# Two transformer blocks with a routed mixture of experts: the experts' weights dealt to the partitions in runs of 16 and 8 KB

## The reference, cut to what matters

```python
h2 = _rms(x, norm2_g[l]) * (1.0 + sc2[:, None, :]) + sh2[:, None, :]
x = x + g2[:, None, :] * _hier_moe(h2, w_rg[l], b_rg[l], w_re[l], b_re[l], w1[l], w3[l], w2[l])

def _hier_moe(h, w_rg, b_rg, w_re, b_re, w1, w3, w2):
    g_logits = hf @ w_rg + b_rg          # 4 groups
    e_logits = hf @ w_re + b_re          # 16 experts, 4 in a group
    ...                                  # best group, best two of its experts, softmax weights
    for e in range(N_EXPERTS):
        he = jax.nn.silu(hf @ w1[e]) * (hf @ w3[e])
        y = y + combine[:, e:e + 1] * (he @ w2[e])
```

## Time and profile before

| | |
|---|---|
| median of 3 runs | 1717.02 us (1716.3 to 1721.85) |
| the profiled execution, its own time | 1726.32 us |
| its span, first to last instruction | 1724.5 us |
| mean granted TensorE clock | 0.978 |
| PE / DVE / ACT / POOL busy | 94% / 40% / 15% / 6% |
| HBM read / written | 355.02 MB / 15.48 MB |

### The profile page before, as it was taken

How to read it: one execution, slowest core, us unless ns; L and a number is a source line. 1 busy time by engine, 2 the same in 40 slices (tenths; PEclk the granted TensorE clock), 3 DMA queues, 4 the chain that set the end, 5 groups by cost and what they waited for, 6 DMA issues and landing times.

```text
span 1724.5 us, 17356 instructions
## 1 busy us (share of the span) xinstructions
PE 1626.6 (94%) x6960; PEld 878.5 (51%) x6960; DVE 697.5 (40%) x1322; ACT 256.0 (15%) x576; POOL 108.3 (6%) x123
## 2 busy tenths in 40 slices
PE   4999999999999999999989999999989958998997
PEld 2445556474444444446756788448855633333332
DVE  1617853468886000112264765004484342111112
ACT  3121113010000000000154110000222311011110
POOL 1000001100000000001000100001131110110101
PEclk9999999999999999999989999999999978999999
DMA  9452441146665321107610699424623449999996
GB/s 340 169 195 99 146 165 56 49 147 219 214 225 207 135 98 49 49 1 257 225 50 1 229 333 363 175 98 154 197 98 122 147 178 354 390 392 391 391 387 254
DMA packets 160623, 333.94 MB, mean 194 GB/s; under 512 B 15288, under 2 KB 15568, under 8 KB 160544
## 3 DMA queue, kind: packets, MB, share of 16 engines
q1 hardware_dynamic: 141408, 298.90, 47.7%
q0 software_dynamic: 18224, 30.78, 5.5%
q10 hardware_dynamic: 912, 3.17, 0.5%
HBM read 355.02 MB, written 15.48 MB: 215 GB/s over the span
## 4 chain that ended last, share of the span: by engine, by line
PE 88%; DMA 4%; DVE 4%; issue 2%; POOL 1%; ACT 1%; SPq 0%; DVEq 0%; ACTq 0%; POOLq 0%
PE psum L624 85%; PE psum L628 4%; DMA wring<-in_ev_w_in 2%; DMA wring<-in_w_mod 1%; DMA wring<-in_mlp_w 1%; ACT wide L1663 0%; POOL small L1523 0%; DVE wide L2068 0%; DVE big L2401 0%; DMA x_slots<-wide,slot_i 0%; DVE big L2560 0%; DMA big<-x_slots 0%; DVE small L2559 0%; POOL x_slots L1609 0%; DVE small L2183 0%
## 5 line engine op out<-in xcount | busy, mean ns | idle before, releaser
L624 PE MATMUL psum<-wring,big 128*128 128x512 f32 (+2 forms) x1600 | 559.6, 579 | 13.8 <-issue 13.3
L624 PE MATMUL psum<-wide,wring 128*128 128x256 f32 (+3 forms) x1872 | 490.2, 437 | 0.2
L624 PEld LDWEIGHTS psum<-wring,big 128*128 128x128 f32 (+1 forms) x1600 | 242.8, 173 | 310.1 <-issue 306.1
L624 PEld LDWEIGHTS psum<-wide,wring 128*128 128x128 f32 (+1 forms) x1872 | 304.3, 184 | 173.0 <-issue 144.6
L624 PE MATMUL psum<-wring,wide 128*128 128x512 f32 (+3 forms) x576 | 216.1, 576 | 9.0 <-DMA wring<-in_w_mod 5.4
L1663 ACT ACTIVATE big<-psum 128x512 f32<-128x512 f32 (+2 forms) x155 | 83.0, 546 | 665.0 <-PE psum L624 614.3
L2068 DVE SCALAR_TENSOR_TENSOR wide<-wring,csilu,wide 128x512 f32<-128x512 f32 x252 | 175.5, 748 | 3.0
L624 PEld LDWEIGHTS psum<-wring,wide 128*128 128x128 f32 (+1 forms) x576 | 97.7, 188 | 109.2 <-issue 96.0
L2168 DVE TENSOR_TENSOR wide<-psum,gate 128x512 f32<-128x512 f32 x27 | 18.7, 691 | 325.2 <-PE psum L624 325.0
L1523 POOL TENSOR_TENSOR small<-small 128x1 f32<-128x1 f32 (+2 forms) x30 | 41.1, 1372 | 1037.8 <-DVE small L2185 884.7
L1663 ACT ACTIVATE wide<-psum 128x256 f32<-128x256 f32 (+2 forms) x114 | 46.0, 418 | 313.3 <-PE psum L628 158.9
(11 more groups left out here) (266 smaller groups left out, 885.5 us busy)
## 6 DMA issues: line engine op xcount, KB each, us to landing
wring<-in_mlp_w SPq DMA_DIRECT2D x32, 2048.0 KB, 8.7
wring<-in_w SPq DMA_DIRECT2D x32, 2048.0 KB, 21.9
wring<-in_w_mod SPq DMA_DIRECT2D x24, 2048.0 KB, 13.0
big<-in_w SPq DMA_DIRECT2D x23, 2048.0 KB, 20.6
wide<-in_w SPq DMA_DIRECT2D x14, 2048.0 KB
wring<-in_w_ada SPq DMA_DIRECT2D x12, 2048.0 KB, 8.6
wring<-in_w_in SPq DMA_DIRECT2D x8, 2048.0 KB, 8.4
wring<-in_ev_w_in SPq DMA_DIRECT2D x6, 2048.0 KB, 13.0
```

The costliest lines, as they stand in the source:

```text
L624: return nc.tensor.matmul(o, a, b, start=first, stop=last)
```

## The change

The rows of D are dealt to the partitions in another order: partition p gets the rows 8p to 8p + 7 (`(p k) n -> p k n`) of w1 and w3, one run of 16 KB, and of w2, for each half of the 512 inner rows, the two rows 2p and 2p + 1, a run of 8 KB. So that sums run over matching rows, the tokens' columns (`rms_row(t, True)`), the router weights, the modulation (`modp`, a copy of 16 columns of `modc` made through DRAM) and the inner rows `he` take the same order. The core of the diff:

```diff
+        modp = sb("modp", [P, 2, KC])
+        modp_scratch = nc.dram_tensor("modp_scratch", [2, D], F32, kind="Internal").ap()
+            def by_halves(w):
+                return w.rearrange("p (h c) n -> p h c n", h=2)
@@ load_up
-  sp.dma_start(w13_ring[e % 2][:, w], src[0, e].rearrange("(k p) n -> p k n", p=P)).then_inc(...)
+  sp.dma_start(w13_ring[e % 2][:, w], src[0, e].rearrange("(p k) n -> p k n", p=P)).then_inc(...)
@@ load_down
-  sp.dma_start(w2_ring[:, e % 2], I["w2_2"][0, e].rearrange("(f p) n -> p f n", p=P)).then_inc(...)
+  sp.dma_start(by_halves(w2_ring[:, e % 2]), I["w2_2"][0, e].rearrange("(h p c) n -> p h c n", h=2, c=2)).then_inc(...)
@@ load_spill_up, load_spill_down: the same
@@ gpsimd, after pool.wait_ge(x_ready, 12)
+  pool.wait_ge(modc_ready, 4)
+  for j in range(2):
+      pool.dma_start(modp_scratch[j].rearrange("(k p) -> p k", p=P), modc[:, 2, 24 + 8 * j:32 + 8 * j, 0],
+                     allow_slow_non_contiguous=True).then_inc(modp_out, 16)
...
-  (wr[:, :, 0:4], I["w_rg_2"][0].rearrange("(k p) n -> p k n", p=P)),
-  (wr[:, :, 4:20], I["w_re_2"][0].rearrange("(k p) n -> p k n", p=P)),
+  (wr[:, :, 0:4], I["w_rg_2"][0].rearrange("(p k) n -> p k n", p=P)),
+  (wr[:, :, 4:20], I["w_re_2"][0].rearrange("(p k) n -> p k n", p=P)),
...
+  pool.wait_ge(modp_out, 32)
+  pool.dma_start(modp[:, :, :], modp_scratch.rearrange("j (p k) -> p j k", p=P)).then_inc(modp_in, 16)
@@ modulate("moe") and modulate_group on ACT and DVE: modp in place of modc, and once
+  act.wait_ge(modp_in, 16)          # and dve.wait_ge(modp_in, 16)
@@ rms_row
-  signal(v_.tensor_scalar(xn[:, t, :], x, lnr, None, ALU.mult), xn_ready)
+  dst = xn[:, t, :]
+  if dealt:
+      dst, x = dst.rearrange("p (k q) -> p k q", k=KC), x.rearrange("p (q k) -> p k q", k=KC)
+  signal(v_.tensor_scalar(dst, x, lnr, None, ALU.mult), xn_ready)
@@ the unit loop on DVE
-  v_.tensor_tensor(he[:, i % 2, :], sg[:, i % 2, :], psum[:, i % 2, T:2 * T], ALU.mult).then_inc(he_ready, 1)
+  v_.tensor_tensor(he[:, i % 2, :].rearrange("p (c q) -> p c q", c=2),
+                   sg[:, i % 2, :].rearrange("p (q c) -> p c q", c=2),
+                   psum[:, i % 2, T:2 * T].rearrange("p (q c) -> p c q", c=2), ALU.mult).then_inc(he_ready, 1)
```

More of the change, by code:

```diff
@@ L484, in build @@
         modc_ready = sem("modc_ready")
+        modp_out = sem("modp_out")
+        modp_in = sem("modp_in")
         gkw_ready = sem("gkw_ready")
@@ L592, in build, with shift_of, scale_of @@
                  "moe": (2, 1, 0, 0, 2, 4)}
+        def shift_of(part, k):
+            l, half, v = PARTS[part][:3]
+            return modp[:, 0, k:k + 1] if (l, half) == (2, 1) else modc[:, l, 24 * half + k, v:v + 1]
+        def scale_of(part, k):
+            l, half, v = PARTS[part][:3]
+            return modp[:, 1, k:k + 1] if (l, half) == (2, 1) else modc[:, l, 24 * half + 8 + k, v:v + 1]
         def banks_of(part):
@@ L1448, in load_up @@
                 for w, src in enumerate((I["w1_2"], I["w3_2"])):
-                    sp.dma_start(w13_ring[e % 2][:, w], src[0, e].rearrange("(k p) n -> p k n", p=P)).then_inc(w13_in[e % 2], 16)
+                    sp.dma_start(w13_ring[e % 2][:, w], src[0, e].rearrange("(p k) n -> p k n", p=P)).then_inc(w13_in[e % 2], 16)
             def load_down(e):
@@ L1694, in modulate @@
                 act.wait_ge(modc_ready, done)
+                if (l, half) == (2, 1):
+                    act.wait_ge(modp_in, 16)
                 width, per = n * P, 4 // n
@@ L1701, in modulate @@
                         last = f(hT[:, k, at:at + width], bank(name)[:, j * width:(j + 1) * width], ACT.Identity,
-                                 bias=modc[:, l, 24 * half + k, v:v + 1], scale=modc[:, l, 24 * half + 8 + k, v:v + 1])
+                                 bias=shift_of(part, k), scale=scale_of(part, k))
                     free(last, name)
@@ L1986, in modulate_group @@
                     last = f(slots_of(g)[:, k, :], psum[:, 4, k * P:(k + 1) * P], ACT.Identity,
-                             bias=modc[:, 2, 24 + k, 0:1], scale=modc[:, 2, 32 + k, 0:1])
+                             bias=modp[:, 0, k:k + 1], scale=modp[:, 1, k:k + 1])
                 last.then_inc(hs_ready, 1)
@@ L2140, in modulate @@
                 l, half, v, at, n, done = PARTS[part]
+                if (l, half) == (2, 1):
+                    dve.wait_ge(modp_in, 16)
                 width, per = n * P, 4 // n
@@ L2147, in modulate @@
                         last = v_.tensor_scalar(hT[:, k, at:at + width], bank(name)[:, j * width:(j + 1) * width],
-                                                modc[:, l, 24 * half + 8 + k, v:v + 1],
-                                                modc[:, l, 24 * half + k, v:v + 1], ALU.mult, ALU.add)
+                                                scale_of(part, k), shift_of(part, k), ALU.mult, ALU.add)
                     free(last, name)
@@ L2200, in head_rate, with rms_row @@
                 root(v_.tensor_scalar(out_rate, out_rate, 1.0 / width, eps, ALU.mult, ALU.add), out_rate)
-            def rms_row(t):
+            def rms_row(t, dealt=False):
                 x = xres[:, X0 + t, :]
@@ L2725, in _ @@
                     residual(2, "out2", half, (X0 + t,), alpha=1.0)
-                rms_row(t)
+                rms_row(t, True)
             modulate("moe")
@@ L2822, in modulate_group @@
                 for k in range(4, KC):
-                    last = v_.tensor_scalar(slots_of(g)[:, k, :], psum[:, 5, (k - 4) * P:(k - 3) * P], modc[:, 2, 32 + k, 0:1],
-                                            modc[:, 2, 24 + k, 0:1], ALU.mult, ALU.add)
+                    last = v_.tensor_scalar(slots_of(g)[:, k, :], psum[:, 5, (k - 4) * P:(k - 3) * P], modp[:, 1, k:k + 1],
+                                            modp[:, 0, k:k + 1], ALU.mult, ALU.add)
                 last.then_inc(hs_ready, 1)
```

6 lines of the change are left out of this document (3 added, 3 removed).

## The result

| | before | after |
|---|---|---|
| median, same chip | 1718.57 us (1716.3 to 1721.85, 4 runs) | 1749.41 us (1748.72 to 1753.6, 4 runs) |
| ratio | | 1.0173, 95% interval 1.0145 to 1.02 |
| profiled execution / its span | 1726.32 / 1724.5 us | 1748.72 / 1746.9 us |
| mean granted TensorE clock | 0.978 | 0.972 |

Slower by 1.7%, where 0.6% faster was forecast. The page of the profile after: TensorE's line, DMA share and GB/s by slice, the packets, and two of the costliest groups.

What follows compares the result with a forecast made beforehand. TensorE was taken to bound most of the kernel, nearly level with DMA in the experts' stretch. Weight waits -10.7 us and strided pass +0.5 gave -10.2 from 1717.02: 1706.8 us, 0.6% faster, range 1703 to 1721.

Steps and rivals of the forecast that it cites:

- The bound and its relief: Experts' stretch: TensorE needs 247.3 us, DMA takes 259; longer runs remove most of 11.7 us of weight waits, -10.7 us.
- the straight line through 2 and 4 KB: DMA packet cost in the experts' stretch: 11.1 ns fixed plus 73.6 ns for each 2 KB.
- The rival: Experts' stretch: long weight packets hold up the short packets of ysb's store; +14 us, 1731 us, chance 0.14.
- the same 30.0: Experts' stretch: q0's 10.09 MB and what they disturb take 30.0 us of DMA time, before and after alike.
- 21.5 us as the point from which it decides: Experts' stretch: store landing time beyond which VectorE waits; 23 us for two units less 1.5 for work and issue.
- The unit of 13.25 us: Experts' stretch: time of a unit if stores landed in 25 us, against 12.07; 25 us over 21 units.
- the 11 us taken off for a lag: Experts' stretch: VectorE may lag 11 us once before TensorE notices, subtracted from 25 us to give +14.
- The tokens' order: Last pass of `rms_row` reads `x` at a stride of 8 elements: +0.5 us once, bounds 0 and +1.8.
- The inner rows: `he` in the experts' loop reads at a stride of 2 elements; covered even at three times its time: 0.
- GpSimd's stream: Modulation copy ahead of the root for `ikd`: issues 2.5 us later, cover 5.3, so 0; upper end 3.5 us, chance 0.07.
- The tail: After the experts: last pieces of TensorE and VectorE unchanged, the last store only quicker: 0.

Runs made afterwards that it cites:

- e1: Changed kernel with loads of w1, w3 and w2 cut to 4 KB runs, old store of ysb kept; 1719.48 us, ratio 0.9988 to the kernel before.
- e4: Changed kernel with loads of w1 and w3 cut to 8 KB runs, w2 left at 8 KB, old store; 1721.1 us, ratio 1.0005 to the kernel before.
- e3: Changed kernel, long runs kept, with the store of ysb issued as two plain DMAs; 1711.14 us, ratio 0.9951 to the kernel before.
- b1: Kernel before the change with only the store of ysb issued as two plain DMAs; 1716.21 us, ratio 0.9957 to the kernel before.
- e2: Changed kernel with w1 and w3 cut to 2 KB runs and w2 to 4 KB, old store; 1729.68 us, ratio 1.0038 to the kernel before.
- h1: Changed kernel, long runs, two plain stores, modulation copy moved later on GpSimd; 1713.27 us, ratio 0.9944 to the kernel before; repeat 1710.81 us, 0.9929.
- h2: Changed kernel with 4 KB runs, two plain stores and the modulation copy moved later on GpSimd; 1711.16 us, ratio 0.9924 to the kernel before.

## Why the prediction was wrong

**The bound and its relief: right.** TensorE and DMA were nearly level, and with dealt weights the waits for w1 and w3 go from the stretch (11.7 us to none). Its worth of -10.7 us was reached by no run through the dealing alone: e1 and e4 gain 5.3 and 5.8 us with the old store, e3 gains 5.7 over b1. e3's stretch is 13.4 us shorter than before, and 7.7 of these are the store's, which relieves the same waits. Packets of 16 KB took 611 ns and of 8 KB 309 (medians of the packets' records; forecast 600 and 305.5), so the straight line through 2 and 4 KB held.

**The rival was the mechanism, and the step that failed is its dismissal.** In the sum GpSimd's queue stands with "the same 30.0" us and nothing for a later landing ("what is late next is nothing on the DMA side"; "the store can only be quicker"). What the runs showed in place of that 0: a store lands in 22.7 us at the median of all 21, up to 36.6, instead of 12.6, and the experts' stretch grows by 23.8 us, of which the plain store takes back all (e3). The prediction had the effect whole: one to one turns, some 30 small packets, 21.5 us as the point from which it decides. It gave it 0.14 with "the turns are few where q1 runs dry" and "q1's 21 packets a unit can't hold up 36 turns all the way". The first of these was half right: q1 does run dry, but only after TensorE has stood still. And an average over a unit says nothing of the moment of a store: q1 had 97.3% of the engines beside the small packets, since a load that lands 15.2 us after its issue at some 400 GB/s has about three loads of 2 MB in flight. The landing was forecast at 22.7 us, and the first store landed in just that, its small packets taking 14.4 us where 13.6 were forecast; already 22.7 was over the threshold of 21.5, and that alone should have carried more than 0.14. It also wasn't asked what the small packets were: 433 beside 552 is far more than the 64 that a store of 256 KB needs at 4 KB each.

**The size of the rival's term: +14 forecast, +23.8 measured in the stretch.** The unit of 13.25 us in the prediction is worked out from a landing of 25 us, for which it gives no source; from its own 22.7 the same step, (22.7 + 1.5) / 2, gives 12.1, no more than the 12.07 of before. The 20 intervals between the first and the last stored unit measure (1718.5 - 1453.1) / 20 = 13.27:

```profile
L1651 POOL DMA_DIRECT2D y_slots<-lnb x21: 798/808/872, 1453.1 to 1718.5; - x21
...
DMA to landing us min/median/max: 8.7/22.7/36.6
```

That this agrees with 13.25 is luck: the median landing is 22.7, and e4, with 22.3, has a unit of (1695.6 - 1458.6) / 20 = 11.85. The unit is not one steady loop through the store, as the prediction has it. The landings rise store by store, to 36.6 at the worst, each store coming while the one before is still under way, and TensorE pays in three halts (9.8 us at 1533, 1.9 and 6.5 before 1620, 1.8 and 7.1 before 1700). That the rise comes from the stores and token groups standing behind each other in GpSimd's queue is my reading; no run isolates it. Nor does VectorE's lag carry through to the end: its last four units wait for TensorE alone. So the 11 us taken off for a lag were the wrong kind of term; each halt costs TensorE, and its lower clock behind it costs again. On TensorE's side the 23.8 us stand as 18.0 of idling and 5.9 of slower matmuls. From 1441 us on it waits 13.6 us for token groups in the same queue (landing at 26.6, not foreseen), 13.5 for VectorE's half of the groups' modulation (L2853), and 2.4 in two smaller waits, less the 11.7 that went. The medians differ by 30.8 us and the spans by 22.4, as the profiled execution of before was itself 7.8 us above its median of 1718.57.

**The tokens' order: +0.5 forecast, +0.4 measured.** The second token norm and TensorE behind it, as the earlier trace rows:

```profile
1393.36 1.14 DVE L2238 TENSOR_SCALAR wide<-xres,small 128x1024 f32<-128x1024 f32 x1 [0.67 <-POOL small L1541]
...
1394.56 3.67 PE L642 MATMUL psum<-const,wide 128*128 128x128 f32 x16 [4.95 <-DVE wide L2238]
```

1.14 against 0.75 us; TensorE idles 4.95 instead of 4.55. The whole price of the stride of 8 is 0.39 us for 1024 columns, below the bound of +1.8. The Trainium skill, SBUF — State Buffer, section Door 1, has strides beyond 4 elements pay for each element; the trace agrees in the sign.

**The inner rows: 0, and they are free.** A stride of 2 elements costs nothing: 417 ns, as before.

```profile
L2866 DVE TENSOR_TENSOR wide<-wide,psum 128x256 f32<-128x256 f32 x23 | 9.6, 417 | 94.0 <-ACT wide L1687 94.0
```

**GpSimd's stream: 0 forecast with an upper end of 3.5; not settled, 0.6 to 6.5.** The issues were priced nearly right (2.2 us for the scatters, 1.9 forecast), but the scatter lands after 9 us, between the rows of 5.3 and 12.6; with the middle of these, 9, the cover of 5.3 us is used up, which the sum could have had. `ikT` is 0.6 us later than in before and TensorE waits 2.05 us for it, the intervals differ by 4.7 on average, and e2's 0.38% are 6.5 us. The sum asked only whether the gap is covered, not what a gap does to the clock of the matmuls behind it.

**The tail: 0.** Nothing there moved of its own. In after the last three stores land in 9.2, 12.1 and 8.7 us, so the tail is late only because TensorE is.

## What to carry to other kernels

Before weight runs are made longer, look at what shares the DMA engines with them: count the packets of the smaller transfer (not its bytes), multiply by the time of one long packet, and compare with the time that its buffer gives. Do it for the longest run of stores and loads in that queue, not for the median one. A transfer that is off the critical path with 2 KB neighbours can be on it with 16 KB ones, so its slack has to be worked out again. And try 4 KB first: with the plain store it had all of the gain here, and with the old store it kept the turns short.

## What the runs showed of the hardware that was not expected

- A GpSimd store of 128 partitions x 2 KB through a three-dimensional DRAM pattern left 448 records of 8 bytes beside its data; as two plain DMAs of 64 partitions it left none and landed in 5.4 us instead of 12.6 (before), and in 6.5 instead of 25.8 (after).
- Between two busy queues an engine took turns one packet at a time: 32 to 35 weight packets an engine went by during the first store's small packets, whether they were of 2 KB (3.3 us) or of up to 4, 8 or 16 KB (6.3, 10.5, 14.4 us).
- A GpSimd scatter of 1024 pieces of 4 bytes to DRAM landed 8.8 to 9.7 us after its issue (in h1 and h2, later in the program, 10.6 to 12.7), and held up its queue: the load of `w_rg`, with as many pieces, landed in 9.3 us behind it and in 3.4 without it.
